# Attention in groups of three quads, row maxima masked on VectorE, one round of ones-products a block

## The chip, the cores and the metric

The kernel runs on one core of a Trainium2 chip. Its time is the device time of one execution in microseconds (us), the median of several executions. Before the change it is 3550.74 us over 3 runs (3547.54 to 3555.72). The profile comes from one further execution.

## The reference

One inference step of a small decoder. The part that matters here is the causal attention over the prompt: 4096 positions, 8 heads of 64 channels, float32. For a query t and a key s not after it the logit is

```python
s = einsum('bqhd,bkhd->bhqk', q, k) * ATTN_SCALE
s = s + (fq[..., :, None] - fk[..., None, :])   # sums of the log forget gates
s = where(k_pos <= q_pos, s, -inf)
p = softmax(s, axis=-1)
out = einsum('bhqk,bkhd->bqhd', p, v)
```

Around it stand the input projection, the attention of the decode step over a paged cache, a pooling branch with gates, and the output projection with two norms. The change leaves all of these as they are.

## The kernel before

The program is a row of phases: projection, decode attention, prompt attention (phase_attend), gates, merge. Only phase_attend is touched. There each engine has its own instruction list, written out by Python loops, and semaphores tie the lists together.

The queries of a head are cut into 8 rows of 512; a (head, row) pair is a **block**, 64 in all. Block row j sees j + 1 key tiles of 512. One key tile of one block is a **quad** (288 in all), and the last quad of a block lies on the diagonal. A quad is two **steps** of two key groups of 128.

For each quad the engines do this:

- **Units** (TensorE L1031, VectorE L971). For each of the 4 query groups of 128 a matmul puts 128 x 512 logits into one of two banks of the tile mx, and VectorE reduces the bank to its row maximum. On the diagonal the unit is 128 to 512 columns wide, and a second matmul (L1034, identity times the triangle tri) adds the mask. There are 1152 units, 256 of them on the diagonal. A unit may be written when the reduction of the unit two before is done (bank_free). Units run ahead of the block that needs them. When a block's units are done VectorE combines their maxima (L978), and TensorE spreads them over a row (L1041) that goes into the scores as a shift.
- **Scores** (L1060, L1061, on the diagonal also the mask L1064): the transposed logits, one key group at a time, into st. ScalarE takes the exponential into probs (L914, L918), a ring of 8 steps.
- **Weighing** (L1081): probabilities times v, accumulated over the block in o_ps.
- **Sums** (GpSimd L880, L881, L883 to L886). The four key groups of a quad are added to one 128 x 512 tile in quad_sum. Two neighbouring quads of a block become one (L865). What is left are the **kept** sums: 1, 1, 2, 2, 3, 3, 4, 4 for the rows 0 to 7, 160 in all.
- **Totals** (function total, L1093). For every kept sum, four products with ones add over the partitions into a bank of mx, which takes its turn among the units' banks. VectorE copies the result (L984).

The order on TensorE is written in groups of 2 quads, 144 groups: 8 halves of scores with units between them at fixed places (units_after; a group without a diagonal quad takes up to 9 units, one with a diagonal quad up to 7), then the spread for blocks that start in the next group, then the 4 weighings, then the totals of the blocks that ended a group earlier. VectorE and ScalarE follow the same groups. Float32 products of probabilities and of sums show as two MATMUL records each.

Of the kernel before, what the change touches and what calls it, by code (L numbers as in the profile page):

```python
# [23 lines left out]
ALU = mybir.AluOpType  # L24
# [593 lines left out]
def phase_attend(nc, io, keep):  # L618
# [6 lines left out]
    RING = 8  # L625
    SUMS = 12
# [6 lines left out]
    MASKS_READY = 17  # L633
# [15 lines left out]
    NGROUP = NQUAD // 2  # L649
    start_group = [quad_base[b] // 2 for b in range(NB)]  # L650
    end_group = [(quad_base[b + 1] - 1) // 2 for b in range(NB)]
# [10 lines left out]
    def most_units(g):  # L662
        return 7 if g >= quad_base[NT] // 2 and (on_diagonal(2 * g) or on_diagonal(2 * g + 1)) else 9
# [14 lines left out]
    def units_after(g, place):  # L678

        units = units_in(g)  # L680
        if len(units) > 8:
            return units[place:place + 1]
        skipped = 8 - len(units)
        at_end = 4 if on_diagonal(2 * g) else 8
        places = [p for p in range(1, 9) if p != at_end][:len(units)] if skipped == 1 else list(range(1, 1 + len(units)))
        return [k for k, p in zip(units, places) if p == place]
# [6 lines left out]
    def summed_with_next(n):  # L693

        c = n - quad_base[block_of[n]]
        return c % 2 == 0 and c < row(block_of[n])

# [14 lines left out]
    with ExitStack() as ctx:  # L712
# [7 lines left out]
        tri_raw = m.sb("tri_raw", [P, P])  # L720
        tri_t_raw = m.sb("tri_t_raw", [P, 2 * P])
        tri = m.sb("tri", [P, P], F32R)
# [6 lines left out]
        quad_sum = m.sb("quad_sum", [P, SUMS, TILE])  # L729
# [27 lines left out]
        summed = m.sem("summed")  # L757
        sum_chain = m.sem("sum_chain")
# [9 lines left out]
        def _(sp):  # L768
# [57 lines left out]
            for g in range(NGROUP):  # L826
                for b in (ending(g - 1) if g >= 1 else []):
                    store_o(b)
                for b in (ending(g - 2) if g >= 2 else []):
                    store_den(b)  # L830
                while q_next < NB and end_group[q_next - AHEAD] <= g - 1:
                    load_q(q_next)
                    q_next += 1
                b = block_of[2 * g]
# [16 lines left out]
        def _(pool):  # L851
            nc.gpsimd.memset(tri_raw[:], 0.0)
            nc.gpsimd.memset(tri_t_raw[:], 0.0).then_inc(tri_ready, 1)
            pool.wait_ge(tri_ready, 1)
            nc.gpsimd.affine_select(out=tri_raw[:], in_=tri_raw[:], compare_op=ALU.is_ge, fill=-BIG, base=0,
# [5 lines left out]
            def end(n, last):  # L861

                if n > quad_base[block_of[n]] and summed_with_next(n - 1):
                    chain.link(last)
                    last = nc.gpsimd.tensor_tensor(quad_sum[:, n % SUMS], quad_sum[:, n % SUMS], quad_sum[:, (n - 1) % SUMS], ALU.add)  # L865
                last.then_inc(summed, 1)

            def add_quad(n):

                b = block_of[n]  # L870
                out = quad_sum[:, n % SUMS]
                first, second = probs[:, 2 * n % RING], probs[:, (2 * n + 1) % RING]
                pool.wait_ge(exp_done, 2 * n + 2)
                if n >= SUMS:
                    pool.wait_ge(bank_ready, bank_of["den", block_of[n - SUMS]] + 1)
# [16 lines left out]
        def _(act):  # L892
# [31 lines left out]
            for g in range(NGROUP):  # L924
                for b in (ending(g - 1) if g >= 1 else []):
                    copy_o(b)
                for s in range(4 * g, 4 * g + 4):
# [7 lines left out]
        def _(dve):  # L935
# [22 lines left out]
            link(nc.vector.tensor_copy(tri[:], tri_raw[:]))  # L958
# [7 lines left out]
            def unit(k):  # L966
# [3 lines left out]
                dve.wait_ge(bank_ready, n + 1)  # L970
                nc.vector.tensor_reduce(max_parts[:, b % AHEAD, t, c:c + 1], mx[:, n % 2, 0:width], AX_X, ALU.max).then_inc(bank_done, 1)  # L971

            def combine(b):
# [4 lines left out]
                nc.vector.tensor_reduce(shift_w[:, b % 2, :, HD], max_parts[:, b % AHEAD, :, 0:j + 1], AX_X, ALU.max, negate=True).then_inc(shift_ready, 1)  # L978

# [12 lines left out]
            for g in range(NGROUP):  # L992
# [7 lines left out]
                for k in units:  # L1000
                    if k >= needed:
                        unit(k)
                for b in dens_after(g):
                    copy_den(b)
            for b in ending(NGROUP - 1):
# [3 lines left out]
        def _(pe):  # L1009
# [9 lines left out]
            def unit(k):  # L1019
                b, t, c = unit_at(k)  # L1020
                h, j = head(b), row(b)
                if k == unit_base[b]:
# [3 lines left out]
                    if j % 2 == 0:  # L1026
# [17 lines left out]
            def scores(s, half):  # L1044
# [3 lines left out]
                if half == 0:  # L1048
                    if s % 4 == 0 and starting(s // 4):
                        pe.wait_ge(shift_copied, starting(s // 4)[-1] + 1)  # L1050
# [34 lines left out]
            def total(b):  # L1085

                pe.wait_ge(summed, quad_base[b + 1])
                n = bank_of["den", b]
                bank_free(n)
                quads = [q for q in range(quad_base[b], quad_base[b + 1]) if not summed_with_next(q)]  # L1090
                for q in quads:
                    for t in range(TT):
                        last = nc.tensor.matmul(mx[t * 32:(t + 1) * 32, n % 2, 0:P], keep["ones"][:, 0:32], quad_sum[:, q % SUMS, t * P:(t + 1) * P],  # L1093
                                                start=(q == quads[0]), stop=(q == quads[-1]))
# [6 lines left out]
            for g in range(NGROUP):  # L1101
                for k in units_after(g, 0):
                    unit(k)
                for place in range(8):
                    scores(4 * g + place // 2, place % 2)
                    for k in units_after(g, place + 1):
                        unit(k)
                if starting(g + 1):
                    pe.wait_ge(exp_done, 4 * g + 3)
                for b in starting(g + 1):  # L1110
                    spread_shift(b, starting(g + 1)[0])
                for s in range(4 * g, 4 * g + 4):
# [1105 lines left out]
```

## Time and profile before

| | |
|---|---|
| median of 3 runs | 3550.74 us |
| profiled execution: time | 3556.43 us |
| profiled execution: span | 3554.8 us |
| prompt attention in it | about 1097 to 2545 us |
| granted TensorE clock in 1400 to 2400 us | 1.00 of full speed |

The span runs from the first to the last instruction. The trace gives each instruction a start and a duration. Matmuls overlap in the records (a 512 column matmul shows 0.40 us, while the next one starts 0.23 us after it), so what one costs is read from start to start. PE is TensorE's matmuls, PEld its weight loads, DVE is VectorE, ACT ScalarE, POOL GpSimd.

### The profile page before, as it was taken

To read this page: it belongs to the slowest core of one execution; us is meant where nothing else is said; L and a number is where in the kernel's file an instruction comes from. 1 tells how busy PE (TensorE), PEld (TensorE's weight loads), DVE (VectorE), ACT (ScalarE), POOL (GpSimd) and SP (SyncE) were. 2 spreads that over 40 slices of the span, in tenths; PEclk is the share of its full clock that TensorE was granted. 3 is DMA by queue.
4 is the path that set the end of the run, shared out by engine and by line. 5 is a ranking of instruction groups with operands and counts; after the bars stand their busy time and mean duration, and the time that the engine had idled before them with its cause. 6 is when DMAs were issued, how large, how long until landed. Compare 5 with 4: busy or idle time off the path is not lost. (4 is left out here: it accounts for less than half of the span.)

```text
span 3554.8 us, 49146 instructions
## 1 busy us (share of the span) xinstructions
PE 3303.2 (93%) x17744; PEld 2365.7 (67%) x17744; DVE 1627.9 (46%) x2596; ACT 1126.3 (32%) x1532; POOL 1338.1 (38%) x1273
## 2 busy tenths in 40 slices
PE   8999999696964999999999999999799999959998
PEld 5777777572813666666666666666488888848876
DVE  3333332361615555555555555555343543445554
ACT  4222222141411444444444444454421121111111
POOL 0000000133331787788888888888600000000000
PEclk9999999797985999999999999999899999979999
DMA  5333443599987114141413131410311111055664
GB/s 182 132 125 128 142 158 113 173 365 366 367 312 143 44 37 87 36 89 35 86 37 85 37 85 37 85 33 11 112 72 47 47 68 74 24 183 182 206 206 155
DMA packets 239929, 435.41 MB, mean 122 GB/s; under 512 B 63544, under 2 KB 107577, under 8 KB 237664
## 3 DMA queue, kind: packets, MB, share of 16 engines
q1 hardware_dynamic: 216327, 362.34, 33.5%
q0 software_dynamic: 20768, 68.17, 5.1%
q10 hardware_dynamic: 2656, 2.62, 0.2%
q8 instruction: 101, 1.65, 0.2%
q14 instruction: 77, 0.62, 0.1%
HBM read 314.19 MB, written 119.03 MB: 122 GB/s over the span
## 5 line engine op out<-in xcount | busy, mean ns | idle before, releaser
L971 DVE TENSOR_REDUCE at_max_parts<-at_mx 128x1 f32<-128x512 f32 (+3 forms) x1152 | 737.0, 647 | 410.5 <-PE at_mx L1031 284.6
L914 ACT ACTIVATE at_probs<-at_st,at_gap 128x1024 f32<-128x1024 f32 x448 | 498.6, 1115 | 511.4 <-PE at_st L1061 511.1
L880 POOL TENSOR_TENSOR at_pair_sum<-at_probs 128x1024 f32<-128x1024 f32 x224 | 531.5, 2373 | 196.2 <-ACT at_probs L914 179.7
L1081 PE MATMUL at_o_ps<-at_probs,at_v 128*64 128x512 f32 (+3 forms) x2304 | 499.9, 566 | 0.0
L1031 PE MATMUL at_mx<-at_k_one,at_q_top 71*128 71x512 f32 (+3 forms) x1152 | 461.3, 402 | 14.0 <-DMA at_k_all<-scratch_k_parts 7.9
L1060 PE MATMUL at_st<-at_q_all,at_k_all 128*128 128x512 f32 (+3 forms) x1152 | 459.1, 399 | 6.9 <-ACT at_probs L918 5.6
L1061 PE MATMUL at_st<-at_q_one,at_k_one 67*128 67x512 f32 (+3 forms) x1152 | 440.1, 382 | 0.0
L1081 PEld LDWEIGHTS at_o_ps<-at_probs,at_v 128*64 128x64 f32 x2304 | 171.7, 137 | 246.4 <-issue 184.2
L93 PE MATMUL ga_acc<-ga_h_high,ga_w_high 128*128 128x512 f32 x768 | 299.8, 390 | 0.0
L95 PE MATMUL ga_acc<-ga_h_high,ga_w_low 128*128 128x512 f32 x768 | 299.6, 390 | 0.0
L94 PE MATMUL ga_acc<-ga_h_low,ga_w_high 128*128 128x512 f32 x768 | 299.6, 390 | 0.0
L881 POOL TENSOR_TENSOR at_quad_sum<-at_pair_sum 128x512 f32<-128x512 f32 x224 | 286.2, 1278 | 17.6
L1031 PEld LDWEIGHTS at_mx<-at_k_one,at_q_top 71*128 71x128 f32 x1152 | 221.2, 192 | 97.8 <-issue 41.7
L1060 PEld LDWEIGHTS at_st<-at_q_all,at_k_all 128*128 128x128 f32 x1152 | 220.1, 191 | 77.3 <-issue 43.0
L1061 PEld LDWEIGHTS at_st<-at_q_one,at_k_one 67*128 67x128 f32 x1152 | 220.5, 191 | 36.8
L1597 POOL MEMSET mg_minus_half<- 128x1 f32 x1 | 0.1, 98 | 583.9 <-POOLq L66 583.9
L93 PE MATMUL mg_acc<-mg_w_high,mg_mix_high 128*128 128x512 f32 x512 | 201.1, 393 | 5.2 <-DVE mg_x L1668 5.2
L93 PE MATMUL pj_acc<-pj_h_high,pj_w_high 128*128 128x512 f32 x512 | 202.9, 396 | 1.1 <-DVE pj_kv_rows L459 0.8
L95 PE MATMUL mg_acc<-mg_w_high,mg_mix_low 128*128 128x512 f32 x512 | 200.6, 392 | 0.0
L94 PE MATMUL mg_acc<-mg_w_low,mg_mix_high 128*128 128x512 f32 x512 | 200.3, 391 | 0.0
L296 POOL TENSOR_TENSOR pj_rms<-pj_squares,pj_eps_sum 128x1 f32<-128x1 f32 (+1 forms) x33 | 7.3, 221 | 511.2 <-ACT pj_junk L314 499.3
L95 PE MATMUL pj_acc<-pj_h_high,pj_w_low 128*128 128x512 f32 x512 | 199.6, 390 | 0.0
(318 smaller groups left out, 4957.7 us busy)
## 6 DMA issues: line engine op xcount, KB each, us to landing
dc_pages<-in_cache_k_dram SPq DMA_DIRECT2D x128, 256.0 KB, 5.3
dc_pages<-in_cache_k_dram POOLq DMA_DIRECT2D x128, 256.0 KB, 5.3
dc_pages<-in_cache_v_dram SPq DMA_DIRECT2D x128, 256.0 KB, 8.1
dc_pages<-in_cache_v_dram POOLq DMA_DIRECT2D x128, 256.0 KB, 5.4
scratch_h_t<-pj_h_t SPq DMA_DIRECT2D x8, 2048.0 KB
scratch_q_parts<-pj_stage SPq DMA_DIRECT2D x32, 512.0 KB, 3.4
scratch_k_parts<-pj_stage SPq DMA_DIRECT2D x32, 512.0 KB, 2.8
at_q_all<-scratch_q_parts SPq DMA_DIRECT2D x128, 128.0 KB
```

Of the source, the lines that this page charges most:

```text
L93: nc.tensor.matmul(out, lhs_high, rhs_high, start=first, stop=False)
L94: nc.tensor.matmul(out, lhs_high, rhs_low, start=False, stop=False)
L95: return nc.tensor.matmul(out, lhs_low, rhs_high, start=False, stop=last)
L296: chain.link(nc.gpsimd.tensor_tensor(out, squares[0:rows, n:n + 1], eps_sum[0:rows], ALU.add))
L880: chain.link(nc.gpsimd.tensor_tensor(pair, first, second, ALU.add))
L881: end(n, nc.gpsimd.tensor_tensor(out, pair[:, 0], pair[:, 1], ALU.add))
L914: nc.scalar.activation(probs[:, s % RING], st[:, s % 2], ACT.Exp, bias=bias).then_inc(exp_done, 1)
L971: nc.vector.tensor_reduce(max_parts[:, b % AHEAD, t, c:c + 1], mx[:, n % 2, 0:width], AX_X, ALU.max).then_inc(bank_done, 1)
L1031: last = nc.tensor.matmul(mx[:, n % 2, 0:width], q_top[0:KM, b % AHEAD, t * P:(t + 1) * P], k_one[h % 2][0:KM, c * TILE:c * TILE + width], ...
L1060: nc.tensor.matmul(out, k_all[h % 2][:, keys], q_all[:, b % AHEAD, at:TILE], start=True, stop=False)
L1061: last = nc.tensor.matmul(out, k_one[h % 2][0:KR, keys], q_one[0:KR, b % AHEAD, at:TILE], start=False, stop=(c < j))
L1081: last = nc.tensor.matmul(o_ps[half * HD:(half + 1) * HD, b % 2, at:TILE], v[:, h % 2, 4 * c + own], probs[:, s % RING, half, at:TILE], st ...
```

## The change

Five things change together in phase_attend.

1. A group has three quads (QUADS = 3): 12 halves of scores, up to 13 units, or 12 where a diagonal quad is in it, then 6 weighings. There are 96 groups in place of 144. The ring of probs has 12 steps.
2. The mask of a diagonal unit leaves TensorE. VectorE adds the triangle and takes the maximum in one tensor_tensor_reduce, written back in place in PSUM.
3. VectorE adds a block's kept sums (join, 128 x 512 float32, both inputs in SBUF), 96 additions. A group's joins stand behind its units and wait for GpSimd's sums of the group before.
4. total makes one round of four products a block, 64 rounds in place of 160, and waits for the last join.
5. The sums have 6 slots for kept quads and one for the others, and GpSimd's waits follow that.

```diff
-    RING = 8
-    SUMS = 12
+    QUADS = 3
+    STEPS = 2 * QUADS
+    RING = 2 * STEPS
+    SUMS = 6
...
     def most_units(g):
-        return 7 if g >= quad_base[NT] // 2 and (on_diagonal(2 * g) or on_diagonal(2 * g + 1)) else 9
+        return 4 * QUADS if g >= quad_base[NT] // QUADS and any(on_diagonal(QUADS * g + i) for i in range(QUADS)) else 4 * QUADS + 1
...
+                if c == row(b):
+                    nc.vector.tensor_tensor_reduce(out=mx[:, n % 2, 0:width], in0=mx[:, n % 2, 0:width], in1=tri[:, TILE - width:TILE], scale=1.0,
+                                                   scalar=NO_MAX, op0=ALU.add, op1=ALU.max,
+                                                   accum_out=max_parts[:, b % AHEAD, t, c:c + 1]).then_inc(bank_done, 1)
+                    return
...
+            def join(n):
+                dve.wait_ge(summed, n + 1)
+                if joined_by(n) >= 2:
+                    dve.wait_ge(joined, joined_by(n) - 1)
+                before = kept[kept.index(n) - 1]
+                nc.vector.tensor_tensor(quad_sum[:, sum_slot(n)], quad_sum[:, sum_slot(n)], quad_sum[:, sum_slot(before)], ALU.add).then_inc(joined, 1)
+
+            def join_after(g):
+                for n in joins:
+                    if n // QUADS == g - 1:
+                        join(n)
...
+                join_after(g)
                 for b in dens_after(g):
                     copy_den(b)
...
                 last = nc.tensor.matmul(mx[:, n % 2, 0:width], q_top[0:KM, b % AHEAD, t * P:(t + 1) * P],
-                                        k_one[h % 2][0:KM, c * TILE:c * TILE + width], start=True, stop=(c < j))
-                if c == j:
-                    last = nc.tensor.matmul(mx[:, n % 2, t * P:width], ident_r[:], tri[:], start=False, stop=True)
+                                        k_one[h % 2][0:KM, c * TILE:c * TILE + width], start=True, stop=True)
...
-                pe.wait_ge(summed, quad_base[b + 1])
+                q = quad_base[b + 1] - 1
+                if q in joins:
+                    pe.wait_ge(joined, joined_by(q))
+                else:
+                    pe.wait_ge(summed, q + 1)
...
+                for t in range(TT):
+                    last = nc.tensor.matmul(mx[t * 32:(t + 1) * 32, n % 2, 0:P], keep["ones"][:, 0:32], quad_sum[:, sum_slot(q), t * P:(t + 1) * P],
+                                            start=True, stop=True)
```

Two places show what moves. The first is TensorE around the total of a long block, where four kept sums were multiplied. Before (L1031 unit, L1034 its mask, L1081 weighing, L1093 total):

```order
L1031 MATMUL at_mx<-at_k_one,at_q_top 128x512
L1060 MATMUL at_st<-at_q_all,at_k_all 128x512
L1061 MATMUL at_st<-at_q_one,at_k_one 128x512
L1081 MATMUL at_o_ps<-at_probs,at_v 64x512 x8
L1093 MATMUL at_mx<-at_quad_sum,keep_ones 32x128 x16
L1031 MATMUL at_mx<-at_k_one,at_q_top 128x384
L1034 MATMUL at_mx<-at_tri,at_ident_r 128x128
L1060 MATMUL at_st<-at_q_all,at_k_all 128x512
```

And with the change, around another total (the same operations now stand on L1066, L1093, L1094, L1114 and L1128):

```order
L1093 MATMUL at_st<-at_q_all,at_k_all 128x512
L1094 MATMUL at_st<-at_q_one,at_k_one 128x512
L1066 MATMUL at_mx<-at_k_one,at_q_top 128x512
L1114 MATMUL at_o_ps<-at_probs,at_v 64x512 x12
L1128 MATMUL at_mx<-at_quad_sum,keep_ones 32x128 x4
L1093 MATMUL at_st<-at_q_all,at_k_all 128x512
```

Sixteen ones-products became four, eight weighing products in a row became twelve, and no mask stands behind a unit.

The second place is VectorE's list. Before, it holds reductions (L971), combines (L978) and copies of totals (L984):

```order
L971 TENSOR_REDUCE at_max_parts<-at_mx 128x1 x7
L984 COPY at_den_out<-at_mx 128x128
L978 TENSOR_REDUCE at_shift_w<-at_max_parts 128x4
L971 TENSOR_REDUCE at_max_parts<-at_mx 128x1 x7
L984 COPY at_den_out<-at_mx 128x128
```

With the change (L992 is the plain reduction, L988 the masked one, L1006 a join, L1017 the copy of a total, L999 a combine):

```order
L988 ISA at_mx,at_max_parts<-at_mx,at_tri 128x256
L988 ISA at_max_parts 128x1
L992 TENSOR_REDUCE at_max_parts<-at_mx 128x1 x2
L988 ISA at_mx,at_max_parts<-at_mx,at_tri 128x384
L988 ISA at_max_parts 128x1
L992 TENSOR_REDUCE at_max_parts<-at_mx 128x1
L1006 TENSOR_TENSOR at_quad_sum<-at_quad_sum 128x512
L1017 COPY at_den_out<-at_mx 128x128
L999 TENSOR_REDUCE at_shift_w<-at_max_parts 128x4 x2
```

A masked maximum is two instructions on VectorE, the operation and a read of its result, and the join stands between the group's units and the copy of the total.

## Rows read from the trace of the kernel before

**Rows 1.** The page: span, busy time, share, instructions of TensorE and VectorE.
```profile
span 3554.8 us, 49146 instructions
PE 3303.2 (93%) x17744; PEld 2365.7 (67%) x17744; DVE 1627.9 (46%) x2596; ACT 1126.3 (32%) x1532; POOL 1338.1 (38%) x1273
```

**Rows 2.** Windows: one stretch of the attention, columns as in its first row.
```profile
core 0: us, PE busy (x) PEld busy (x) DVE busy (x) ACT busy (x) POOL busy (x), PEclk, DMA share, GB/s
2000.00:2200.00 200.00, 198.47 (x1103) 128.62 (x1103) 107.65 (x182) 100.76 (x124) 161.56 (x122) 1.00 0.25 58
```

**Rows 3.** Groups by line and shape, attention only: the 512 column units.
```profile
L1031 PE MATMUL at_mx<-at_k_one,at_q_top 71*128 71x512 f32 x944 | 390.2, 413 | 0.0
```

**Rows 4.** Timeline (start us, duration us, engine, line), TensorE: unit with and without mask.
```profile
2000.09 0.40 PE L1031 MATMUL at_mx<-at_k_one,at_q_top 71*128 71x512 f32 x1
...
2000.33 0.22 PE L1034 MATMUL at_mx<-at_tri,at_ident_r 128*128 128x128 f32 x1
...
2000.39 0.45 PE L1060 MATMUL at_st<-at_q_all,at_k_all 128*128 128x512 f32 x1
...
2000.68 0.40 PE L1061 MATMUL at_st<-at_q_one,at_k_one 67*128 67x512 f32 x1
...
2001.62 0.40 PE L1031 MATMUL at_mx<-at_k_one,at_q_top 71*128 71x512 f32 x1
...
2001.85 0.40 PE L1060 MATMUL at_st<-at_q_all,at_k_all 128*128 128x512 f32 x1
...
2002.09 0.40 PE L1061 MATMUL at_st<-at_q_one,at_k_one 67*128 67x512 f32 x1
2002.09 0.19 PEld L1031 LDWEIGHTS at_mx<-at_k_one,at_q_top 71*128 71x128 f32 x1
2002.32 0.39 PE L1031 MATMUL at_mx<-at_k_one,at_q_top 71*128 71x512 f32 x1
```

**Rows 5.** Timeline: totals of one kept sum and of two, each with what follows.
```profile
2044.62 0.43 PE L1093 MATMUL at_mx<-at_quad_sum,keep_ones 128*32 128x128 f32 x8
...
2044.97 0.50 PE L1031 MATMUL at_mx<-at_k_one,at_q_top 71*128 71x512 f32 x1
...
2054.77 0.65 PE L1093 MATMUL at_mx<-at_quad_sum,keep_ones 128*32 128x128 f32 x16
2055.35 0.50 PE L1060 MATMUL at_st<-at_q_all,at_k_all 128*128 128x512 f32 x1
```

**Rows 6.** Timeline: from the last unit of a group over the weighing to the next group.
```profile
2002.64 3.65 PE L1081 MATMUL at_o_ps<-at_probs,at_v 128*64 128x512 f32 x16
...
2003.98 0.14 PEld L1081 LDWEIGHTS at_o_ps<-at_probs,at_v 128*64 128x64 f32 x2 [0.29 <-ACT at_probs L914]
2004.41 0.14 PEld L1081 LDWEIGHTS at_o_ps<-at_probs,at_v 128*64 128x64 f32 x2 [0.28 <-issue]
...
2006.22 0.50 PE L1060 MATMUL at_st<-at_q_all,at_k_all 128*128 128x512 f32 x1
...
2006.57 0.39 PE L1061 MATMUL at_st<-at_q_one,at_k_one 67*128 67x512 f32 x1
```

**Rows 7.** Timeline: nine reductions in a row; weight load of an early unit.
```profile
2045.51 6.47 DVE L971 TENSOR_REDUCE at_max_parts<-at_mx 128x1 f32<-128x512 f32 x9
```
```profile
1126.83 0.29 PEld L1031 LDWEIGHTS at_mx<-at_k_one,at_q_top 71*128 71x128 f32 x1 [0.46 <-DVE at_max_parts L971]
```

**Rows 8.** Groups by line and shape: nearest operations to the masked maximum.
```profile
L971 DVE TENSOR_REDUCE at_max_parts<-at_mx 128x1 f32<-128x512 f32 x960 | 659.9, 691 | 306.0 <-PE at_mx L1031 284.6 <-PE at_mx L1034 3.1
...
L1394 DVE TENSOR_TENSOR ga_stage<-ga_acc,ga_stage 128x512 f32<-128x512 f32 x32 | 22.1, 692 | 155.5 <-ACT ga_stage L1303 150.8 <-DVE ga_pooled L1387 4.3
...
L483 DVE TENSOR_TENSOR_SCAN pj_f_e<-keep_ones,pj_f_z 8x512 f32<-8x512 f32 x8 | 9.7, 1212 | 0.3
```
```profile
L1629 ACT ACTIVATION_READ_ACCUMULATOR mg_junk<-mg_x 128x1 f32 x32 | 6.0, 187 | 0.0
```

**Rows 9.** The same view: an addition of two SBUF tiles on VectorE; GpSimd's longest addition.
```profile
L1330 DVE TENSOR_TENSOR ga_h_low<-ga_h_t,ga_h_high 128x512 fp32r<-128x512 f32 x64 | 43.0, 691 | 2.3 <-ACT ga_h_high L1278 2.3
```
```profile
L880 POOL TENSOR_TENSOR at_pair_sum<-at_probs 128x1024 f32<-128x1024 f32 x224 | 531.5, 2373 | 196.2 <-ACT at_probs L914 179.7 <-POOL at_quad_sum L865 8.3 <-POOL at_quad_sum L881 7.8
```

More of the change, by code:

```diff
@@ L632, in phase_attend @@
     SPREAD_READY = 12
-    MASKS_READY = 17
+    MASKS_READY = 16
+    NO_MAX = -3.0e38
     def head(b):
@@ L647, in phase_attend @@
     unit_base = [TT * quad_base[b] for b in range(NB + 1)]
-    NGROUP = NQUAD // 2
-    start_group = [quad_base[b] // 2 for b in range(NB)]
-    end_group = [(quad_base[b + 1] - 1) // 2 for b in range(NB)]
+    NGROUP = NQUAD // QUADS
+    start_group = [quad_base[b] // QUADS for b in range(NB)]
+    end_group = [(quad_base[b + 1] - 1) // QUADS for b in range(NB)]
     def on_diagonal(n):
@@ L680, in units_after @@
         units = units_in(g)
-        if len(units) > 8:
+        if len(units) > 2 * STEPS:
             return units[place:place + 1]
-        skipped = 8 - len(units)
-        at_end = 4 if on_diagonal(2 * g) else 8
-        places = [p for p in range(1, 9) if p != at_end][:len(units)] if skipped == 1 else list(range(1, 1 + len(units)))
+        places = [1 + i * 2 * STEPS // len(units) for i in range(len(units))]
         return [k for k, p in zip(units, places) if p == place]
@@ L696, in summed_with_next, with sum_slot, joined_by @@
         return c % 2 == 0 and c < row(block_of[n])
+    kept = [n for n in range(NQUAD) if not summed_with_next(n)]
+    def sum_slot(n):
+        return SUMS if summed_with_next(n) else kept.index(n) % SUMS
+    joins = [n for n in kept if kept.index(n) and block_of[kept[kept.index(n) - 1]] == block_of[n]]
+    def joined_by(n):
+        return len([q for q in joins if q <= n])
     def dens_after(g):
@@ L870, in add_quad @@
                 b = block_of[n]
-                out = quad_sum[:, n % SUMS]
+                out = quad_sum[:, sum_slot(n)]
                 first, second = probs[:, 2 * n % RING], probs[:, (2 * n + 1) % RING]
                 pool.wait_ge(exp_done, 2 * n + 2)
-                if n >= SUMS:
-                    pool.wait_ge(bank_ready, bank_of["den", block_of[n - SUMS]] + 1)
+                if not summed_with_next(n) and kept.index(n) >= SUMS:
+                    old = kept[kept.index(n) - SUMS]
+                    if kept[kept.index(old) + 1] in joins:
+                        pool.wait_ge(joined, joined_by(kept[kept.index(old) + 1]))
+                    else:
+                        pool.wait_ge(bank_ready, bank_of["den", block_of[old]] + 1)
                 if n + 1 < quad_base[b + 1]:
@@ L926, in _ @@
                     copy_o(b)
-                for s in range(4 * g, 4 * g + 4):
+                for s in range(STEPS * g, STEPS * g + STEPS):
                     exps(s)
@@ L1085, in total @@
             def total(b):
-                pe.wait_ge(summed, quad_base[b + 1])
+                q = quad_base[b + 1] - 1
+                if q in joins:
+                    pe.wait_ge(joined, joined_by(q))
+                else:
+                    pe.wait_ge(summed, q + 1)
                 n = bank_of["den", b]
                 bank_free(n)
[L1090 to L1094, printed above, removed]
+                for t in range(TT):
+                    last = nc.tensor.matmul(mx[t * 32:(t + 1) * 32, n % 2, 0:P], keep["ones"][:, 0:32], quad_sum[:, sum_slot(q), t * P:(t + 1) * P],
+                                            start=True, stop=True)
                 last.then_inc(bank_ready, 1)
@@ L1103, in _ @@
                     unit(k)
-                for place in range(8):
-                    scores(4 * g + place // 2, place % 2)
+                for place in range(2 * STEPS):
+                    scores(STEPS * g + place // 2, place % 2)
                     for k in units_after(g, place + 1):
```

24 lines of the change are left out of this document (12 added, 12 removed).

## The prediction

> **What bounds the kernel now.** I read the page's busy shares first, then the windows of the attention, then the groups by line there, and last the timeline of single groups. The page has TensorE busy for 93% of a span of 3554.8 us [rows 1]. In the attention, the only phase that changes, it is busy 198.5 of 200 us at the full granted clock, against 107.7 us on VectorE and 161.6 us on GpSimd [rows 2]. The 512 column units have 0.0 us of idle time in front of their matmuls, so in steady state TensorE does not wait for the reductions that free its banks [rows 3]. So a microsecond of TensorE time taken out is a microsecond of the kernel, as long as no other engine becomes late.
>
> How late VectorE already is has to be read before its list is made longer. A half of scores with one unit takes TensorE 0.70 us, from the unit at 2001.62 to the next at 2002.32 [rows 4]. Nine reductions in a row take 6.47 us with 0.69 us each, so one every 0.72 us [rows 7, 8]. That is slower than the units come. The average share of 54% hides it, because VectorE rests while TensorE weighs. What saves the kernel before is that a burst has only 9 units, or 7 with a diagonal quad, and each diagonal unit gives VectorE extra time through its mask.
>
> **What leaves TensorE.** Masks: from a masked unit to the second score matmul behind it are 0.59 us (2000.09 to 2000.68), without a mask 0.47 us (2001.62 to 2002.09) [rows 4]. That is 0.12 us for each of the 256 masks, 31 us in all. Half of it is the mask's own stream, half the weight load behind it, which a short matmul does not cover.
>
> Totals: one kept sum takes 0.35 us up to the next matmul, two take 0.58 us, so each further sum costs 0.23 us [rows 5]. 160 sums become 64, and 96 x 0.23 = 22 us.
>
> Groups: a group pays three times for its turn from scores to weighing and back. The weighing starts 0.32 us after the last unit where the stream has 0.23 us, 0.09 us more [rows 4, 6]. Its 8 pairs of records come 0.43 us apart, 3.44 us, but the next scores start 3.58 us after its start, 0.14 us more. The first score matmul then takes 0.35 us to the next, 0.12 us more [rows 6]. Together 0.35 us, and 48 groups fewer give 17 us. The sum of the three is 70 us.
>
> **What is added, and where it lies.** The masked maximum has no row before. From below it is the plain reduction of the same width, nothing extra (691 ns at 512 columns; a PSUM and SBUF addition also takes 692) [rows 8]. A gain below that I exclude, since the same columns pass through the same engine. From above it is a two-input VectorE operation that runs at 1212 ns for 512 columns, plus a result read like ScalarE's of 187 ns, 0.71 us extra at full width [rows 8]; the mean diagonal width is 320 columns, so 0.33 + 0.19 = 0.52 us. I take 0.15 us extra, near the addition's row with most of a read. It is an estimate from these rows.
>
> The Trainium skill (VectorE: DVE Perf Modes, section Two Vector instructions with no wait between them) says that an operation that also writes out its accumulator is two instructions. The instruction order shows this for the masked maximum; no run here has timed the second one on VectorE.
>
> The cost on TensorE comes through the two banks. A unit's weights, loaded 0.23 us ahead of its matmul [rows 4], must wait until the reduction of the unit two before is done. Take a group of 13 units without a diagonal quad. The first reduction starts 0.54 us after the first unit's matmul when a total's copy is in front (2044.97, 2045.51) [rows 5, 7]. Eleven reductions are done at 0.54 + 11 x 0.72 = 8.46 us, so the last unit may start at 8.69 us. TensorE by itself would be there after 12 x 0.70 + 0.12 = 8.52 us. The two diagonal units it has on average are shorter: TensorE gains 0.09 us on each, VectorE about 0.05 us with the 0.15 us extra. A combine now and then adds 0.2 us. That makes about 0.35 us of waiting, in 40 groups. In the 56 groups with a diagonal quad the scores are shorter by 2 x (0.06 + 0.12 + 0.17) = 0.70 us and their four masks L1064 give back 0.35 us, while 12 units follow each other without the gap that the seven had. VectorE needs about the same 8.4 us up to the last unit, TensorE only 7.8 us: 0.6 us of waiting. The sum is 40 x 0.35 + 56 x 0.6 = 48 us. The same reckoning for the 9 unit groups of before gives 0.54 + 7 x 0.72 + 0.23 = 5.81 us against 8 x 0.70 + 0.12 + one or two masks, 5.9 us, no waiting, as the rows show; it runs a little high, for the first reduction is mostly earlier, so I take 40 us.
>
> Smaller terms. 29 units instead of 24 come before the first group, where TensorE's weight loads wait for reductions (0.46 us in one) [rows 7]: 5 x (0.72 - 0.24) = 2.4 us. A join takes 691 ns [rows 9]. 96 of them, one a group on average, fall into the weighing of 12 x 0.43 = 5.2 us, when VectorE has nothing else. Behind a join wait the copy of a total and the next units; the total on TensorE waits for the block's last join. With one join this is hidden. 32 groups have two. I put 3 us on them, and 3 us on the end, where the last three groups have no units, GpSimd is behind and one more join stands in front of the last total. GpSimd's list is unchanged, and with 2373 ns for its longest addition [rows 9] it stays near 85% of a shorter phase. The larger ring costs nothing.
>
> Sum: -70 + 40 + 2.4 + 3 + 3 = -22 us. Against the profiled execution's own 3556.4 us this is 3534 us. The median of the runs lies 5.7 us lower, so the forecast is 3550.7 - 22 = 3529 us. With the waiting between 25 and 55 us its own range is 3514 to 3544.
>
> **The rivals.** *VectorE keeps up.* If the masked maximum costs hardly more than the plain one and the two banks swallow the lag, the waiting is under 10 us, and the gain is 70 - 8 - 8 = 54 us: 3497 us. For it speaks that units never wait now [rows 3]; against it that 0.72 us is more than 0.70 us and the bursts are a third longer and lose their gaps.
>
> *The masked maximum is dear.* At the upper bound VectorE gets 256 x (0.52 - 0.15) = 95 us more. In groups that already wait, most of it, say 60 us, goes to TensorE: 3529 + 60 = 3589 us, slower by 38. It decides from about 0.28 us extra a diagonal unit, since (0.28 - 0.15) x 256 x 0.65 = 22 us. For it speaks only that it is a form without a row; the nearest two-input row is at 692 ns [rows 8].
>
> *The joins collide with GpSimd.* Both read SBUF tiles at a time when GpSimd is 81% busy [rows 2]. If a join may only run between GpSimd's operations, it waits up to 2.37 us [rows 9]. One a group still fits in 5.2 us. In the 32 groups with two, 0.7 + 0.7 us and one and a half waits of about 2 us fill the weighing; the total and then the next units are late by about 1.2 us, 38 us in all: 3567 us, slower by 16. No row before has such a VectorE operation beside a GpSimd one. The Trainium skill (SBUF - State Buffer, section Who interferes with whom) says that a VectorE instruction with two SBUF inputs contends with a GpSimd instruction that reads SBUF and that the later one is blocked for the whole instruction. By that rule this rival's waits happen; it says nothing on whether they reach TensorE. The masked maximum has one input in PSUM, and the same section has it free of this.
>
> That the change doesn't do what it says I exclude: the order shows masks and products gone.
>
> **How the numbers follow.** The forecast case gets 0.56, VectorE keeps up 0.17, the dear maximum 0.15, the collision 0.12. A measurement can tell 0.2%, 7 us, from no change. The forecast case is faster in 0.50 and within 7 us in 0.06; the first rival is faster; the dear maximum is slower in 0.13 and same in 0.02, the collision slower in 0.10 and same in 0.02. Faster 0.67, same 0.10, slower 0.23. The range 3495 to 3570 takes in the full gain and the collision, and leaves out the upper bound of the dear maximum.
>
> **What would show it.** The windows of the attention should get shorter by some 25 us, with TensorE's busy share a little lower than 99%. The row of the unit (L1066) should show idle time that ends with VectorE, 25 to 55 us with its weight loads, most of it late in groups. L1128 should have 512 records, L1034's group be gone. The masked maximum should show 0.75 to 0.9 us at 512 columns with its read. Joins of 0.69 us would speak against the collision; joins of 1 to 3 us, or GpSimd additions grown by 0.7 us, for it. I am wrong if units wait less than 20 us (then it is faster than I say) or if TensorE waits for joins at the totals.

## The result, and the profile after

In one comparison on the same chip the changed kernel takes 3500.80 us, median of 4 runs (3492.80 to 3505.21), and the kernel before 3553.23 us, median of 4 runs (3547.54 to 3557.71). The ratio is 0.9851 with a 95% interval of 0.9827 to 0.9875: 52 us faster. The forecast was 3529 us. The time is that of the rival *VectorE keeps up*, 3497 us.

The page of the kernel after, against [rows 1]:

```profile
span 3497.7 us, 47532 instructions
PE 3248.9 (93%) x16720; PEld 2318.0 (66%) x16720; DVE 1769.4 (51%) x2947; ACT 1123.4 (32%) x1532; POOL 1371.3 (39%) x1273
```

The span is 57.1 us shorter, TensorE has 1024 records fewer (256 masks, 768 halves of ones-products), VectorE is busy 141 us more, and GpSimd, whose list is the same, 33 us more. From the start of the attention's first matmul to the end of its last are 1447.4 us before (1097.36 to 2544.81) and 1390.5 us after (1093.77 to 2484.26). The 57 us all lie there: what stands before the attention is 3.6 us shorter and what follows it 3.4 us longer, and neither was changed.

The window of the attention, against [rows 2]:

```profile
core 0: us, PE busy (x) PEld busy (x) DVE busy (x) ACT busy (x) POOL busy (x), PEclk, DMA share, GB/s
2000.00:2200.00 200.00, 199.39 (x1022) 126.79 (x1019) 131.92 (x238) 101.49 (x121) 173.15 (x126) 1.00 0.32 69
```

TensorE is not less busy, as I had expected, but more: 199.4 of 200 us. The groups by line and shape show where each engine's time goes in the steady part of the attention, 1130 to 2490 us (busy us, mean ns, idle us before them and what ended it), against [rows 3, 5, 8, 9]:

```profile
L992 DVE TENSOR_REDUCE at_max_parts<-at_mx 128x1 f32<-128x512 f32 x880 | 601.8, 690 | 163.0 <-PE at_mx L1066 149.3
L1066 PE MATMUL at_mx<-at_k_one,at_q_top 71*128 71x512 f32 x940 | 392.4, 417 | 1.8 <-DVE at_den_out L1017 1.6
L898 POOL TENSOR_TENSOR at_quad_sum<-at_pair_sum 128x512 f32<-128x512 f32 x224 | 305.5, 1364 | 17.6
L1066 PEld LDWEIGHTS at_mx<-at_k_one,at_q_top 71*128 71x128 f32 x1122 | 212.9, 190 | 83.9 <-DVE at_max_parts L992 15.3 <-issue 13.7 <-DVE at_den_out L1017 3.7
L1006 DVE TENSOR_TENSOR at_quad_sum<-at_quad_sum 128x512 f32<-128x512 f32 x96 | 141.8, 1478 | 28.1 <-POOL at_quad_sum L878 22.7 <-POOL at_quad_sum L903 2.2
L988 DVE CUSTOM_DVE_ANT_0 at_mx<-at_mx,at_tri 128x512 f32<-128x512 f32 x61 | 42.7, 700 | 32.8 <-PE at_mx L1066 31.9
L988 DVE DVE_READ_ACCUMULATOR2_ANT at_max_parts<- 128x1 f32 x243 | 34.3, 141 | 0.0
L1128 PE MATMUL at_mx<-at_quad_sum,keep_ones 128*32 128x128 f32 x512 | 25.8, 285 | 7.1 <-DVE at_quad_sum L1006 7.1
```

The units' matmuls (L1066) wait 1.8 us in all, none of it for a reduction. Their weight loads wait for reductions:

```profile
PEld at_mx L1066 <- DVE at_max_parts L992: 15.3, 84, 0.2
PEld at_mx L1128 <- DVE at_quad_sum L1006: 7.6, 1, 7.6
PE at_mx L1128 <- DVE at_quad_sum L1006: 7.1, 1, 7.1
PEld at_mx L1066 <- DVE at_max_parts L988: 1.7, 7, 0.2
```

(Columns: us in total, times, longest.) A weight load runs beside the matmul in front of it, and most start 0.23 us ahead of their own matmul, so 84 waits of at most 0.2 us can hardly reach the matmuls. The idle time of the matmul rows alone would not prove that, for it misses waits, as the last dose below shows; the sums from start to start further down do. The masked maximum is 700 ns and a read of 141 ns at 512 columns; the join takes 1478 ns where a lone addition took 691; and the only wait for a join on TensorE is one, at the end.

Where the time went, worked out from the records: from the start of each matmul of the attention to the start of the next, summed by what the first one is. So waiting is counted with the matmul in front of it. These sums end at the start of the last matmul, 0.4 us earlier than the stretch above. The last three columns are kernels with one part of the change each; they follow in the next section.

| us | before | after | masks alone | joins alone | groups alone |
|---|---|---|---|---|---|
| units | 282.6 | +18.2 | +11.2 | -0.1 | +2.8 |
| their masks | 28.1 | -28.1 | -28.1 | +0.1 | +0.8 |
| first score matmul | 272.2 | -10.0 | -8.8 | -0.4 | -1.1 |
| second score matmul | 255.8 | +1.8 | -0.4 | -0.2 | +1.4 |
| masks of scores | 37.4 | -11.0 | +3.8 | -0.1 | -12.7 |
| spreads | 22.6 | -0.7 | +0.1 | -0.1 | -1.2 |
| weighing | 495.5 | -6.2 | +0.4 | +2.3 | -7.5 |
| totals | 44.2 | -20.6 | 0.0 | -21.6 | +1.0 |
| sum with setup | 1447.0 | -56.9 | -21.7 | -20.0 | -16.6 |

Most of the +18.2 us of the units lies ahead of the first score matmul, where TensorE waits for reductions before and after: +12.3 us there, for five more units and for the wait that the mask rows held before (8.2 us). Behind it all units together take 274.1 us in place of 268.2, and the growth of the waits for reductions at units is somewhere in these 5.9 us.

### The profile page after: what moved, and what is told of

Read it like the earlier page. It is cut to its first block and busy times, and to the rows that moved or that the text cites. A ratio compares the mean times of both kernels' runs of the same rounds, so it can differ in the third digit from the quotient of the medians.

```text
span 3497.7 us, 47532 instructions
## 1 busy us (share of the span) xinstructions
PE 3248.9 (93%) x16720; PEld 2318.0 (66%) x16720; DVE 1769.4 (51%) x2947; ACT 1123.4 (32%) x1532; POOL 1371.3 (39%) x1273
## 5 line engine op out<-in xcount | busy, mean ns | idle before, releaser
L992 DVE TENSOR_REDUCE at_max_parts<-at_mx 128x1 f32<-128x512 f32 x896 | 612.6, 690 | 170.8 <-PE at_mx L1066 156.5
L1114 PE MATMUL at_o_ps<-at_probs,at_v 128*64 128x512 f32 (+3 forms) x2304 | 488.8, 563 | 0.0
L1066 PE MATMUL at_mx<-at_k_one,at_q_top 71*128 71x512 f32 (+3 forms) x1152 | 466.7, 407 | 17.5 <-DMA at_k_all<-scratch_k_parts 7.6
L1093 PE MATMUL at_st<-at_q_all,at_k_all 128*128 128x512 f32 (+3 forms) x1152 | 449.4, 390 | 4.3 <-ACT at_probs L931 1.6
L1094 PE MATMUL at_st<-at_q_one,at_k_one 67*128 67x512 f32 (+3 forms) x1152 | 440.7, 383 | 0.0
L1114 PEld LDWEIGHTS at_o_ps<-at_probs,at_v 128*64 128x64 f32 x2304 | 178.8, 137 | 260.7 <-issue 217.7
L898 POOL TENSOR_TENSOR at_quad_sum<-at_pair_sum 128x512 f32<-128x512 f32 x224 | 305.5, 1364 | 17.6
L1066 PEld LDWEIGHTS at_mx<-at_k_one,at_q_top 71*128 71x128 f32 x1152 | 221.4, 192 | 108.9 <-DVE at_max_parts L992 23.6
L1093 PEld LDWEIGHTS at_st<-at_q_all,at_k_all 128*128 128x128 f32 x1152 | 220.4, 191 | 66.5 <-issue 27.4
L1094 PEld LDWEIGHTS at_st<-at_q_one,at_k_one 67*128 67x128 f32 x1152 | 220.7, 192 | 37.2
```

The lines of the kernel that those rows point to most:

```text
L898: end(n, nc.gpsimd.tensor_tensor(out, pair[:, 0], pair[:, 1], ALU.add))
L1066: last = nc.tensor.matmul(mx[:, n % 2, 0:width], q_top[0:KM, b % AHEAD, t * P:(t + 1) * P], k_one[h % 2][0:KM, c * TILE:c * TILE + width], ...
L1093: nc.tensor.matmul(out, k_all[h % 2][:, keys], q_all[:, b % AHEAD, at:TILE], start=True, stop=False)
L1094: last = nc.tensor.matmul(out, k_one[h % 2][0:KR, keys], q_one[0:KR, b % AHEAD, at:TILE], start=False, stop=(c < j))
L1114: last = nc.tensor.matmul(o_ps[half * HD:(half + 1) * HD, b % 2, at:TILE], v[:, h % 2, 4 * c + own], probs[:, s % RING, half, at:TILE], st ...
```

## Experiments: the parts one by one

All kernels below were timed against the kernel before on the same chip; its median moved between 3553 and 3560 us, so ratios are compared.

**Masks alone.** Groups of two quads and the old totals, only the mask moved into the maximum. The two main lines of the edit against the changed kernel:

```diff
-    QUADS = 3
+    QUADS = 2
-    joins = [n for n in kept if ...]
+    joins = []
```

> Groups of two, several rounds of ones-products; only the mask moves to VectorE. Theory A: 0.12 to 0.14 us each of 256 masks, 31 to 36 us faster, 3517 to 3522. Theory B (VectorE is at its limit, the masked maximum is 0.15 us dearer): half of it lost to waits of the units, 3530 to 3540.

Measured: 3532.23 us, ratio 0.9938 (0.9924 to 0.9952), 22 us. The masks' records and the score matmul behind them fall by 36.9 us, but the units take 11.2 us more and the scores' masks 3.8 us more. Of the 11.2 us 8.2 lie ahead of the first score matmul, and that stretch is as long as before (32.1 us against 32.0): a mask gains nothing where TensorE waits for reductions anyway. Elsewhere what a short mask exposed a short unit exposes as well: a score matmul takes 0.289 us behind a mask, 0.287 behind a unit of 128 columns and 0.237 behind one of 512. The time lies in the range of theory B, but its cause is not seen: the units' matmuls wait 3.1 us for reductions, 1.8 us before.

**Joins alone.** Two quads a group, masks on TensorE, one round of ones-products.

> Groups of two as before, masks on TensorE; VectorE joins the kept sums and one round of ones-products is made per block. Theory A (96 rounds at 0.22 us leave TensorE and the joins are hidden): 21 us faster, 3532. Rival (a join waits out GpSimd's running addition, 1.5 us in the mean, and in groups of two it has only 3.4 us of weighing): gain halves, 3540 to 3550, and the totals or the next units show waits for joins.

Measured: 3537.85 us, ratio 0.9954 (0.9941 to 0.9967), 16 us, and 20.0 us in the attention of the profiled execution. The totals give 21.6 us, as computed; 2.3 us come back in the weighing. The rival is half true: joins take 1172 ns on average, but TensorE's matmuls wait for one only, the last (7.7 us, where before it waited 5.5 us for GpSimd):

```profile
L1005 DVE TENSOR_TENSOR at_quad_sum<-at_quad_sum 128x512 f32<-128x512 f32 x96 | 112.5, 1172 | 34.4 <-POOL at_quad_sum L881 31.4 <-POOL at_quad_sum L906 2.2
```

**Groups alone.** Three quads a group, no joins, masks on TensorE. With the 12 slots of before the kept sums do not fit in SBUF beside the longer ring (26624 bytes needed, 24992 left), so this kernel has seven.

> Groups of three quads alone, with 7 slots for kept sums (masks on TensorE, several rounds of ones-products). Theory A (a turn costs about 0.35 us): 17 us faster, and a little more for the places no longer left without a unit. Theory C (the parts add up, and the whole change less the change without groups of three is 12 us): 12 us faster, ratio 0.9966. If turns cost nothing: ratio 1.

Measured: 3543.17 us, ratio 0.9954 (0.9940 to 0.9967), 16 us. The size is the forecast's 17 us, the make-up is not, so the agreement is in part luck: 12.7 us stand at the masks of the scores, and the first score matmuls, which were to give 48 x 0.12 = 5.8 us, give 1.1. In the kernel before, a place without a unit follows the diagonal scores; there the next score matmul waits for ScalarE (median 0.458 us from the scores' mask to it, 30 times). Larger groups have 12 units for 12 places, and that wait goes (0.06 us at the median, 16 times). The weighing gives 7.5 us, where 48 x 0.14 = 6.7 were forecast. The extra for the filled places, 10 us by an expectation written for the version with 12 slots, did not come on top of the 17.

**Fill those places without larger groups.** The kernel before, with 8 units in place of 7 in a group with a diagonal quad.

```diff
-        return 7 if g >= quad_base[NT] // 2 and (...) else 9
+        return 8 if g >= quad_base[NT] // 2 and (...) else 9
```

> The kernel before, with 8 units in a group that has a diagonal quad in place of 7, so no place is left without a unit. Theory (TensorE waits there for ScalarE's exponentials, 0.4 us in 30 groups): about 10 us faster than before, 3543. Rival (the gap gave VectorE its time, and now the units wait for it): same or up to 15 us slower.

Measured: 3555.49 us, ratio 0.9990 (0.9980 to 0.9999), 4 us where 10 were expected. The wait goes (-13.4 us at the scores' masks), but 4.3 us at units, 3.3 at second scores, 2.7 at masks and 1.9 in the weighing come back; 4.2 us are left. Filling the places is not enough by itself.

**Two of the three.** The whole change with two quads a group, and the whole change with the masks back on TensorE.

> Everything of the change but the groups of three. Theory A (parts add up): before minus masks 35 and products 21, 3497, and the groups of three then add another 17 us, which the whole change does not show (3501), so A expects either this to be slower, about 3518, or an interaction. Theory B (in groups of three the waits for VectorE eat what the turns save): 3497 to 3503, equal to the whole change.

> The whole change, but the masks stay on TensorE. If the parts add up, it is slower than the whole change by what the mask alone gains, 22 to 26 us: ratio to before 0.992. If a unit that follows another closely gives the masked maximum away again in groups of three (waits for VectorE), the mask's gain is smaller here: ratio 0.987 to 0.990.

Measured: without the larger groups 3515.46 us, ratio 0.9884 (0.9868 to 0.9901); with the masks on TensorE 3520.12 us, ratio 0.9893 (0.9878 to 0.9908). The singles' gains sum to (0.0062 + 0.0046 + 0.0046) x 3553 = 55 us, the whole gives 53 us. By the sums from start to start they are 21.7 + 20.0 + 16.6 = 58.3 us against 56.9. The parts add up, and nothing large is lost between them. The ratio of the kernel with the masks on TensorE, taken alone, lies where its expectation put waits for VectorE (0.987 to 0.990). But from it to the whole change the attention shrinks by 21.1 us, the 21.7 of the masks alone; and from the kernel without larger groups by 16.0 us, the 16.6 of the groups alone. The ratios are too coarse for that question. The forecast had denied it: it let 40 us of 70 be eaten by VectorE.

## Experiments: does VectorE's pace decide

The forecast took 0.72 us a reduction as VectorE's pace. To test what that pace does, I give VectorE a dose of idle work, a memset that nothing reads, before each of the 1152 reductions of the changed kernel, in four sizes.

```diff
+        idle = m.sb("idle", [P, 4, 1])      # the others: [P, 4, 64]; [P, 4, 200] of bf16; [P, 2, 200]
...
                 dve.wait_ge(bank_ready, n + 1)
+                nc.vector.memset(idle[:, n % 4], 0.0)
```

> The whole change with one more VectorE instruction of about 0.06 us (a memset of one column) in front of every unit's maximum, 1152 times, 69 us of VectorE. Theory A (VectorE keeps up with slack to spare): under 15 us slower than the whole change, below 3515. Theory B (VectorE's pace already ends the bursts): most of it passes on, 45 to 69 us slower, 3546 to 3570.

> The same with a memset of 64 columns, about 0.11 to 0.13 us in front of every maximum, some 130 to 150 us of VectorE. Theory A: slack used up, perhaps 40 us slower. Theory B: 90 to 140 us slower, a straight line through the small dose.

> The whole change with a memset of 200 columns in front of every maximum. The earlier doses show reductions that start 0.61 us apart at their closest, whatever the 0.69 us of their row, and the 64 column memset raised that to 0.62 us only, below the 0.70 us at which TensorE brings units. Theory D (VectorE's pace, start to start, is what counts, and costs nothing below 0.70 us): 200 columns bring it to about 0.76 us, and 1152 units pass on 0.06 us each, 40 to 80 us slower than the whole change. Theory E (VectorE never limits, since it catches up while TensorE weighs): under 10 us slower.

> The whole change, with one memset of 128 x 200 numbers of 4 bytes (into a tile that nothing reads) put on VectorE before each of the 1152 unit reductions. Two theories. D, VectorE's pace decides: a reduction that starts 0.607 us after the one before it, plus the memset (about 0.15 us: one of 100 numbers took 0.142 us, one of 64 took 0.112 us, so 0.20 us for 200), comes to some 0.76 to 0.80 us in plain units and 0.85 to 0.88 us with a mask, more than the 0.70 and 0.75 us that TensorE takes for a unit. VectorE then falls behind and cannot catch up: 1152 x 0.06 to 0.10 us is 70 to 115 us if every unit lies in a run of units, and I expect 40 to 100 us over the 3500.8 us of the whole change, so 3540 to 3600 us, with the wait for the reductions (at the scores and at weight loads) grown by the same sum. E, TensorE never depends on VectorE's pace, only on each reduction's own end: under 15 us over the whole change, as the smaller memsets gave (3 to 11 us).

The pace is read from the trace: the value at which the shortest times from the start of one 512 column reduction to the start of the next one gather. Some 25 of the changed kernel are 0.597 us; for masked reductions without a dose and with the smallest only three are at the value given, the next at 0.700. The attention is the sum from start to start.

| dose | memset, ns | pace, plain | pace, masked | ratio (95%) | attention |
|---|---|---|---|---|---|
| none | | 0.608 us | 0.691 us | 0.9851 (0.9827 to 0.9875) | 1390.1 us |
| 1 column | 59 | 0.611 | 0.698 | 0.9845 (0.9833 to 0.9858) | 1390.9 |
| 64 columns | 112 | 0.619 | 0.707 | 0.9856 (0.9842 to 0.9870) | 1394.5 |
| 200 of 2 bytes | 142 | 0.656 | 0.744 | 0.9866 (0.9851 to 0.9881) | 1401.4 |
| 200 of 4 bytes | 225 | 0.760 | 0.849 | 1.0010 (1.0000 to 1.0020) | 1452.1 |

The first three doses move the pace much less than their own duration, for they lie largely beside the reduction, and they stay below TensorE's 0.70 us a unit [rows 4]. They cost 0.8, 4.4 and 11.3 us in the attention, and their ratios lie within the interval of the change. Two expectations missed here. The 64 columns were to cost 40 us or 90 to 140. The 200 columns of 2 bytes were to bring the pace to 0.76 us and cost 40 to 80 us; they brought it to 0.656, which is why the last dose has 4 bytes. The last goes past 0.70 us, and the whole gain of the change is gone: 3562.71 us, 62 us more in the attention. Its VectorE timeline (start us, duration us):

```profile
1994.62 0.62 DVE L994 TENSOR_REDUCE at_max_parts<-at_mx 128x1 f32<-128x512 f32 x1
1995.24 0.23 DVE L988 MEMSET at_idle<- 128x200 f32 x1
1995.38 0.63 DVE L994 TENSOR_REDUCE at_max_parts<-at_mx 128x1 f32<-128x512 f32 x1
1996.00 0.23 DVE L988 MEMSET at_idle<- 128x200 f32 x1
```

From 1994.62 to 1995.38 are 0.76 us, though a memset and a reduction together show 0.86: the rows overlap. Of the 672 plain reductions of 512 columns that another follows, 601 have it 0.76 us behind them. TensorE's weight loads now wait for every second reduction (1130 to 2490 us), against 84 times and 15.3 us above:

```profile
PEld at_mx L1068 <- DVE at_max_parts L994: 132.4, 538, 0.6
PEld at_mx L1068 <- DVE at_max_parts L990: 21.2, 83, 0.6
```

The matmuls' own row hides most of it:

```profile
L1068 PE MATMUL at_mx<-at_k_one,at_q_top 71*128 71x512 f32 x933 | 427.1, 458 | 3.8 <-DVE at_den_out L1019 1.6 <-DVE at_max_parts L994 0.3
```

It shows 3.8 us of idle time, 1.8 us in the changed kernel. A matmul's record is 0.40 us long and its successor starts 0.23 us behind it, so a late start of under 0.17 us leaves no gap between records. From start to start the units take 42.6 us more than in the changed kernel, the second score matmuls 9.5 and the scores' masks 8.9.

So theory D holds: VectorE's pace decides once it is slower than the units come, and costs little before. With 0.76 us the forecast's own reckoning for a group without a diagonal quad gives 0.54 + 11 x 0.76 + 0.23 = 9.13 us against 8.52, 0.61 us of waiting. With one, the twelfth unit needs ten reductions, four of them 0.089 us dearer: 8.73 us against 7.8. Over 40 and 56 groups that makes an estimate of 76 us; 62 were measured.

## Experiments: joins, the end, and the places of the units

**GpSimd's additions in halves.** The additions of 1024 columns as two of 512, the rest as in the changed kernel.

```diff
-                    chain.link(nc.gpsimd.tensor_tensor(pair, first, second, ALU.add))
+                    for i in range(2):
+                        chain.link(nc.gpsimd.tensor_tensor(pair[:, i], first[:, i], second[:, i], ALU.add))
```

> The whole change, with GpSimd's pair addition of 1024 columns made as two of 512. If a join is blocked until GpSimd's running instruction ends, joins fall from 1478 ns to about 1.2 us in the mean, with none above 1.9 us; if they share bandwidth, the mean stays near 1478 ns. The time stays near 3501 as joins are hidden, or grows by up to 10 us if GpSimd, some 25 us longer, becomes late.

Measured: 3505.78 us, ratio 0.9853 (0.9839 to 0.9867). The joins get shorter, 1137 ns on average in place of 1478 and 859 in place of 1582 at the median, the longest 1.77 us, and the time stays within its interval (the attention of the profiled execution is 4.7 us longer). A join waits for GpSimd's running instruction, and shorter joins make nothing faster. This is how it looks in the changed kernel, two joins in a row beside GpSimd (timelines of the two engines, put together in order of time):

```profile
2055.01 2.37 POOL L897 TENSOR_TENSOR at_pair_sum<-at_probs 128x1024 f32<-128x1024 f32 x1 [0.17 <-PE at_mx L1066]
2056.30 3.31 DVE L1006 TENSOR_TENSOR at_quad_sum<-at_quad_sum 128x512 f32<-128x512 f32 x2
2057.45 1.60 POOL L898 TENSOR_TENSOR at_quad_sum<-at_pair_sum 128x512 f32<-128x512 f32 x1
```

The join is issued at 2056.30 while GpSimd's addition runs until 2057.38. GpSimd's next one takes 1.60 us where the same addition at 2053.56 takes 1.28: it waits for the join. Of the 96 joins 17 take 0.7 us, 73 take 1.6 to 1.9 us and 4 take 2.0 to 2.7 us.

**The end.** The last total waits 7.1 us for the last join, behind GpSimd. In this version TensorE takes the ones-products of the last block's last two quads from their probabilities, and GpSimd and the joins leave them out.

```diff
+    DIRECT = [NQUAD - 2, NQUAD - 1]
...
+                if b == NB - 1:
+                    pe.wait_ge(exp_done, NSTEP)
+                    for s in range(2 * DIRECT[0], NSTEP):
+                        for half in range(2):
...
+                                last = nc.tensor.matmul(mx[t * 32:(t + 1) * 32, n % 2, 0:P], keep["ones"][:, 0:32], probs[:, s % RING, half, t * P:(t + 1) * P],
```

> A version that may beat both: the last two quads of the last block are not summed by GpSimd and joined; TensorE multiplies their probabilities with ones itself (26 products of 128 columns more). The last total then does not wait about 7 us for GpSimd and the last join. Theory: 5 to 6 us faster than the whole change, 3496. If the phase after the attention is bound by something else, no change.

Measured: 3492.95 us, ratio 0.9818 (0.9805 to 0.9831), against 0.9851 for the whole change. The attention is 4 us shorter, and the wait at the last total is gone. It has the lowest time of all versions, but its interval overlaps that of the whole change. The edit reaches the attention alone, and there it gives 4 us. The profiled executions are 12 us apart: 5.3 us lie before the attention and 2.8 behind it, where nothing differs. Over all fifteen kernels the stretch before the attention varies from 1088.5 to 1098.0 us. So no more than the 4 us is shown to come from the edit.

**Thirteen units in every group, on top of it.** Groups with a diagonal quad may take 13 too.

```diff
-        return 4 * QUADS if g >= ... else 4 * QUADS + 1
+        return 4 * QUADS + 1
```

> The version in which the ones-products of the last two quads of a block are taken directly from their probabilities (3492.95 us, 0.9818 of before), with the units of a head handed out thirteen to a group rather than by the table's mix. If the places of the units behind scores and weighing are what is left of TensorE's waiting, the time falls or rises by some 2 to 8 us with them; if the turns between scores and weighing cost the same wherever the units stand, it stays within 2 us of 3493 us. I take the second as the likelier.

Measured: 3508.02 us, ratio 0.9868 (0.9853 to 0.9884): slower by 0.5% than the version before it, more than either expectation. In the attention it is 9 us: 5.4 more at the masks of the scores, 4.3 at the second score matmul and 3.2 at the units, 3.6 less at the first score matmul. TensorE waits for ScalarE where the units have run out:

```profile
PE at_st L1094 <- ACT at_probs L936: 6.2, 14, 0.7
PE at_st L1094 <- ACT at_probs L932: 3.1, 12, 0.3
```

In the changed kernel these two are 1.5 and 1.6 us. I had taken "the places do not matter" as likelier; they do, in a group that has scores and no units to lie between them. That such groups are the ones that wait is argued from the edit and not shown group by group.

## Why the prediction was wrong

**The step that failed** is the term of the waiting: "Nine reductions in a row take 6.47 us with 0.69 us each, so one every 0.72 us [rows 7, 8]. That is slower than the units come." The 0.72 us is not VectorE's pace. It is TensorE's, for each of the nine waited for its unit. In the records the units of this row start 0.70 to 0.71 us apart, but for 0.82 behind the first, which follows a total, and 0.85 behind the one with a mask, and the reductions follow 0.70 to 0.71 us apart, but for two of 0.77 and 0.78 there. So the row's mean of 0.72 holds a mask, and between units it equals TensorE's 0.70. Two signs stood in the same trace. Nine times 0.69 us is 6.22 us, so the row has time in it in which VectorE does not reduce. And where units come closer, on narrow diagonal scores, the reductions follow closer; the VectorE timeline of the kernel before has

```profile
1179.77 1.97 DVE L971 TENSOR_REDUCE at_max_parts<-at_mx 128x1 f32<-128x512 f32 x3 [0.46 <-PE at_mx L1031]
```

which is 1.97 us for three reductions of 0.69 us. They overlap: their starts are 0.608 and 0.673 us apart. After 43 of the 512 column reductions of the kernel before the next one starts within 0.607 to 0.609 us. With 0.608 us in the forecast's reckoning the thirteenth unit of a group may start at 0.54 + 11 x 0.608 + 0.23 = 7.46 us, and TensorE is there at 8.52 us. With a diagonal quad the twelfth may start at 0.54 + 10 x 0.608 + 4 x 0.084 + 0.23 = 7.19 us, and TensorE is there at 7.8. No waiting in either. A lag behind a total's copy or a combine is made good at 0.09 us a unit and need not add up. The reckoning goes by averages and is not good to 10 us: at 0.656 us it still gives no waiting, and that dose cost 11.3 us. The mechanism is real, as the last dose shows; the pace put into it was wrong, and with it the size of the term: 40 us forecast, while the units of the steady part take 5.9 us more in all.

The same step took the weight load 0.23 us ahead of its matmul as fixed. It is not: in the changed kernel the units' loads start 0 to 0.23 us ahead of their matmuls, most often 0.23, and a load that starts up to 0.2 us late still need not delay its matmul.

**Point by point.**

- *Masks, -31 us.* 256 x 0.115 = 29 us by the records behind full units, 22 us in the kernel. The 12 masks or so ahead of the first scores gained nothing, what a short mask exposed a short unit exposes as well, and the scores' masks gave 3.8 us back. Too high by 9.
- *Totals, -22 us.* 20.6 us. Right; rounds of 1 to 4 sums took 356, 574, 792 and 1011 ns, 0.218 us a sum.
- *Groups, -17 us.* 16.6 us. Right in size partly by luck: more than half came by another way, the waits for ScalarE at places without units.
- *The masked maximum, 0.15 us extra.* 0.700 + 0.141 in place of 0.690, start to start some 0.084 us extra. The Trainium skill (VectorE: DVE Perf Modes, section Two Vector instructions with no wait between them) has it as two instructions, and the rows show both. *The masked maximum is dear* is refuted.
- *Early units, +2.4 us.* From the first matmul to the first score matmul it went from 32.0 to 35.9 us, +3.8; the 16.6 us of the groups are net of it.
- *Groups with two joins, +3 us.* Not seen; TensorE waits for one join only.
- *The end, +3 us.* The last total's wait grew from 5.5 to 7.1 us, +1.6.
- *Joins collide with GpSimd.* They do, as the Trainium skill (SBUF - State Buffer, section Who interferes with whom) states: 1478 ns on average, GpSimd's busy time 33 us up. The price of that rival, 38 us, did not come. The joins lie behind the group's units and have the weighing of 5.2 us to themselves. Halving GpSimd's additions changed the joins and not the time.

The measured sizes of the three parts, each with its small costs in it, sum to -21.7 - 20.0 - 16.6 = -58.3 us, against -56.9 us of the whole in the attention.

What the forecast said would prove it wrong, "units wait less than 20 us", is what the profile shows: 1.8 us at the matmuls and 17.0 us for reductions at their weight loads.

## What to carry to other kernels

The spacing of instructions in a burst is the pace of whoever is slower, not the capacity of the engine whose row it is. Look for the shortest start-to-start times of the same operation, where its input was surely ready, before putting a price on a longer burst. Here a consumer that was faster than its producer by 0.09 us an item built up no lag that cost much, and one that was slower by 0.06 us an item lost the whole gain.

Idle time between records shows a wait only if the records do not overlap. Where they do, take the sums from start to start.

A place without filler work between dependent steps is a wait of its own: 0.46 us at the median here, 30 times. Filling it moved most of that wait elsewhere (13.4 us gone, 4.2 us left as gain).

## What the runs showed of the hardware

- Consecutive VectorE instructions overlap. A 512 column reduction from PSUM shows 0.69 us and is followed by the next after 0.608 us at the closest (24 times in the changed kernel after 0.597 or 0.598). With a memset of 59, 112, 142 or 225 ns between the two, the second starts 0.611, 0.619, 0.656 or 0.760 us after the first. So the durations in the rows overstate what a burst takes.
- A join, which reads two SBUF tiles on VectorE, and GpSimd's additions hold each other up: a join that starts under a running addition ends 0.55 us after that one's end (median of 86), and the addition behind grows from 1.28 to 1.60 us.
- A 128 column matmul between 512 column ones costs 0.115 us from start to start, 62 ns of its own and 53 ns at the matmul behind it.
- A 512 column matmul's record is 0.40 us and the next starts 0.23 us behind it. The dose that took 62 us left 3.8 us of idle time in the units' row.
